# Root and reciprocal of the latent norms on one column per token tile, spread by TensorE between two halves of the next projection

## What is computed

```python
def rms_norm(x, g=None):
    xf = x.astype(jnp.float32)
    y = xf * lax.rsqrt(jnp.mean(xf * xf, axis=-1, keepdims=True) + NORM_EPS)
    if g is not None:
        y = y * g.astype(jnp.float32)
    return y.astype(x.dtype)
...
qh = (rms_norm(cq, g_mla_q) @ w_mla_qb).reshape(B, T, MLA_HEADS, MLA_NOPE + MLA_ROPE)
...
kvh = (rms_norm(ckv, g_mla_kv) @ w_mla_kvb).reshape(B, T, MLA_HEADS, MLA_NOPE + MLA_V)
...
k_pe = jnp.broadcast_to(rope_2d(kr[:, :, None, :], tabs_mla), (B, T, MLA_HEADS, MLA_ROPE))
```

## Time and profile before

| | |
|---|---|
| median of 3 runs | 3298.01 us (3291.66 to 3300.49) |
| profiled execution, its own time | 3290.88 us |
| its span, first to last instruction | 3289.1 us |
| PE matmuls busy | 3118.7 us (95%) |
| PE weight loads busy | 2624.0 us (80%, beside the matmuls) |
| DVE busy | 1486.3 us (45%) |
| ACT busy | 1169.0 us (36%) |
| POOL busy | 399.6 us (12%) |
| mean granted clock of TensorE | 0.985 |

### The profile page before, as it was taken

One profiled execution on the slowest core, in us unless ns is written; L12 is line 12 of the kernel. 1 busy time (PEld: TensorE's weight loads), 2 busy tenths in 40 slices (PEclk: granted clock), 3 DMA queues, 4 the chain that ended last, 5 costly groups with the idle time before them and its releaser, 6 DMA issues.

```text
span 3289.1 us, 42671 instructions
## 1 busy us (share of the span) xinstructions
PE 3118.7 (95%) x17576; PEld 2624.0 (80%) x17576; DVE 1486.3 (45%) x2013; ACT 1169.0 (36%) x1709; POOL 399.6 (12%) x304
## 2 busy tenths in 40 slices
PE   6899999999999999999999988999999999999998
PEld 5788888899888877787888867788788877778886
DVE  5555524444436644422222356554455456443334
ACT  3344423444424422211111234443355444332222
POOL 0011100111102201010100100111022112010101
PEclk9999999999999999999999999999999999999999
DMA  4111142111152244124233342223222232422323
GB/s 178 67 54 59 62 139 76 60 59 63 53 175 68 83 135 135 58 88 129 64 122 96 111 134 70 65 64 93 84 78 74 91 121 82 133 83 96 96 96 102
DMA packets 99827, 303.96 MB, mean 92 GB/s; under 512 B 10960, under 2 KB 23376, under 8 KB 99664
## 3 DMA queue, kind: packets, MB, share of 16 engines
q1 hardware_dynamic: 54720, 190.34, 18.1%
q10 hardware_dynamic: 44944, 111.32, 10.2%
HBM read 271.73 MB, written 29.88 MB: 92 GB/s over the span
## 4 chain that ended last, share of the span: by engine, by line
PE 77%; issue 9%; DVE 8%; ACT 4%; POOL 1%; DMA 1%; ACTq 0%; DVEq 0%; POOLq 0%
PE ps L1518 72%; PE ps L1606 2%; PE ps L1644 1%; DVE wl L979 1%; POOL ptl L1500 1%; ACT wh L492 1%; DVE tmp L984 1%; DVE mx L1005 1%; DVE ptl L1020 1%; DVE tmp L1155 1%; DVE hl L1164 0%; PE ps L1722 0%; PE ps L1576 0%; ACT pth L528 0%; ACT prob L540 0%
## 5 line engine op out<-in xcount | busy, mean ns | idle before, releaser
L1518 PE MATMUL ps<-hh,wh 128*128 128x512 f32 x2768 | 831.7, 361 | 41.7 <-DVE wl L979 20.4
L1518 PE MATMUL ps<-hl,wh 128*128 128x512 f32 x2768 | 813.8, 354 | 0.0
L1518 PE MATMUL ps<-hh,wl 128*128 128x512 f32 x2768 | 811.0, 353 | 0.0
L979 DVE TENSOR_TENSOR wl<-raw,wh 128x1024 fp32r<-128x1024 f32 (+2 forms) x356 | 466.0, 1310 | 523.8 <-ACT wh L492 514.3
L1518 PEld LDWEIGHTS ps<-hh,wh 128*128 128x128 f32 x2768 | 451.2, 190 | 127.1 <-issue 35.4
L492 ACT ACTIVATE wh<-raw 128x1024 fp32r<-128x1024 f32 (+2 forms) x356 | 362.2, 1018 | 429.1 <-PE ps L1518 376.4
L1518 PEld LDWEIGHTS ps<-hh,wl 128*128 128x128 f32 x2768 | 451.5, 189 | 77.5
L1518 PEld LDWEIGHTS ps<-hl,wh 128*128 128x128 f32 x2768 | 452.7, 190 | 74.2 <-issue 0.7
L1518 PE MATMUL ps<-yh,wh 128*128 128x512 f32 (+1 forms) x1296 | 403.0, 365 | 14.2 <-DVE yl L1380 5.4
L1518 PE MATMUL ps<-yl,wh 128*128 128x512 f32 (+1 forms) x1296 | 395.5, 359 | 0.0
L1518 PE MATMUL ps<-yh,wl 128*128 128x512 f32 (+1 forms) x1296 | 391.4, 356 | 0.0
(11 more groups left out here) (209 smaller groups left out, 3269.9 us busy)
## 6 DMA issues: line engine op xcount, KB each, us to landing
raw<-in_stream SPq DMA_DIRECT2D x328, 512.0 KB, 3.6
prob<-in_wmod ACTq DMA_DIRECT2D x40, 512.0 KB, 3.6
mraw<-in_wmod ACTq DMA_DIRECT2D x36, 512.0 KB, 3.8
gspill<-prob ACTq DMA_DIRECT2D x32, 384.0 KB, 2.3
tmp<-gspill ACTq DMA_DIRECT2D x24, 384.0 KB, 3.1
early_y<-in_wmod SPq DMA_DIRECT2D x12, 512.0 KB, 14.2
vraw<-gspill ACTq DMA_DIRECT2D x16, 384.0 KB, 3.8
dec<-in_dec ACTq DMA_DIRECT2D x8, 768.0 KB, 4.3
```

What stands on the lines that cost most here:

```text
L979: dve.tensor_tensor(wl[:, s, 0:n], raw[:, s, 0:n], wh[:, s, 0:n].bitcast(F32), ALU.subtract).then_inc(sem("w_lo"), 1)
L1518: ins = pe.matmul(out, lhs[w], rhs[x](cols), start=start and n == 0, stop=stop and n == 2)
```

## The change

The sums of squares go to one column per token tile (`squares`): the 12 matmuls of 128 tokens (8 for layer 1's query) have the squares as weights and one column of ones as the moving side. ACT takes the root of 128 x 6 numbers into `qsc`, DVE their reciprocal. PE spreads the result back over the partitions (`broadcast`): one matmul for each token tile, whose weights are the tile's column repeated 128 times and whose moving side is the identity, into `pair(AUX)`. DVE waits for it (`v_bc`), and its scaling reads `pair(AUX)` in place of `tmp`. PE's program is rewritten: `broadcast` of the query stands between the two halves of chunk 2's projection, `broadcast` of key/value between chunks 4 and 5. Its `squares` for key/value also wait for `v_norm`, since they write where the scaling of the query reads.

```diff
--- before.py
+++ after.py
@@ -143,7 +143,7 @@
             phase("summed", layer, 0, {}, summed, nt=TOK)
             phase("norm", layer, 0, {}, norm, nt=TOK, first=True)
         phase("mla_in", layer, 0, {}, total(
-            {"chunk": 6, "free0": 3, "free1": 2, "v_stat": 2, "v_std": 2, "v_rstd": 2,
+            {"chunk": 6, "free0": 3, "free1": 2, "v_stat": 2, "v_std": 2, "v_rstd": 2, "v_bc": 2,
              "v_norm": 4, "v_hi": 6, "v_lo": 6, "tab": 1}, ROPED))
         head = total({"chunk": 1, "free0": 1}, ROPED)
         att = attention(nq)
@@ -745,7 +745,10 @@
                                            ACT.Square).then_inc(sem(f"free{k}"), 1)
                         if j:
                             split(at, 5)
-                        std(at, j, nt_j, MLA_RANK)
+                        nq = nt_j // P
+                        act.wait_ge(sem("v_stat"), at.v("v_stat", j + 1))
+                        act.activation(qsc[:, j, 0:nq], pair(AUX)[:, 0:nq], ACT.Sqrt, bias=eps[:, :],
+                                       scale=1.0 / MLA_RANK).then_inc(sem("v_std"), 1)
                         if j:
                             split(at, 6)
                         for k in range(RKT):
@@ -1232,13 +1235,16 @@
                                 split(at, 2 * j + k + 1)
                         if j:
                             split(at, 5)
-                        rstd(at, j, nt_j)
+                        nq = nt_j // P
+                        dve.wait_ge(sem("v_std"), at.v("v_std", j + 1))
+                        dve.reciprocal(qsc[:, j, 0:nq], qsc[:, j, 0:nq]).then_inc(sem("v_rstd"), 1)
                         if j:
                             split(at, 6)
+                        dve.wait_ge(sem("v_bc"), at.v("v_bc", j + 1))
                         for k in range(RKT):
                             col = g0 + 2 * KT + j * RKT + k
                             dve.scalar_tensor_tensor(out=tmp[:, k, 0:nt_j], in0=tmp[:, k, 0:nt_j],
-                                                     scalar=gains[:, col:col + 1], in1=tmp[:, 2, 0:nt_j],
+                                                     scalar=gains[:, col:col + 1], in1=pair(AUX)[:, 0:nt_j],
                                                      op0=ALU.mult, op1=ALU.mult).then_inc(sem("v_norm"), 1)
                         for k in range(RKT):
                             dve.wait_ge(sem("v_norm"), at.v("v_norm", 2 * j + k + 1))
@@ -1776,15 +1782,37 @@
                     spread(at, nt)
 
                 elif kind == "mla_in":
-                    for j, nt_j in enumerate((TOK if layer < DEPTH - 1 else LAT, TOK)):
-                        if j == 0 and layer:
-                            project_pair(at, nt_j)
-                        for k in range(RKT if j else 0):
-                            project(at, 2 * j + k, k, j, H, KT, nt_j, whole)
+                    def squares(j, nt_j):
+
                         for k in range(RKT):
                             pe.wait_ge(sem(f"free{k}"), at.v(f"free{k}", j + 1))
-                        stats(at, prob, (0, 1), nt_j, j)
+                        if j:
+                            pe.wait_ge(sem("v_norm"), at.v("v_norm", 2))
+                        for k in range(RKT):
+                            for q in range(nt_j // P):
+                                ins = pe.matmul(pair(AUX)[:, q:q + 1], prob[:, k, q * P:(q + 1) * P], ones[:, 0:1],
+                                                start=k + q == 0, stop=k == RKT - 1 and q == nt_j // P - 1)
+                        ins.then_inc(sem("v_stat"), 1)
+
+                    def broadcast(j, nt_j):
+
+                        pe.wait_ge(sem("v_rstd"), at.v("v_rstd", j + 1))
+                        for q in range(nt_j // P):
+                            ins = pe.matmul(pair(AUX)[:, q * P:(q + 1) * P], qsc[:, j, q:q + 1].to_broadcast([P, P]),
+                                            ident[:, :], start=True, stop=True)
+                        ins.then_inc(sem("v_bc"), 1)
+
+                    nt_q = TOK if layer < DEPTH - 1 else LAT
+                    if layer:
+                        project_pair(at, nt_q)
+                    squares(0, nt_q)
+                    project(at, 2, 0, 1, H, KT // 2, TOK, whole, ktn=KT, done=False)
+                    broadcast(0, nt_q)
+                    project(at, 2, 0, None, H, KT // 2, TOK, whole, kt0=KT // 2, ktn=KT)
+                    project(at, 3, 1, 1, H, KT, TOK, whole)
+                    squares(1, TOK)
                     project(at, 4, 0, 2, H, KT // 2, TOK, whole, ktn=KT, piece=True)
+                    broadcast(1, TOK)
                     project(at, 5, 0, None, H, KT // 2, TOK, whole, kt0=KT // 2, ktn=KT, piece=True)
 
                 elif kind in ("mla_first", "gqa_first"):
```

## The result

The changed kernel takes 3304.35 us (median of 12 runs, 3301.53 to 3309.21) against 3296.93 (12 runs, beside it) for the one before. The medians are 7.4 us apart, 0.23%; the ratio is 1.0027, with a 95% interval of 1.0020 to 1.0034, so the kernel is slower beyond noise, by less than 0.3%, the bound of the forecast's likely cases. The profiled execution has a span of 3300.7 us.

A forecast was written before the change was run, and what follows sets the result against it. TensorE's dense projections were taken to bound the kernel. The chain terms summed to 0.0 us at unchanged clock and clock falls added +3.5, giving 3301.5 us on the median of 3298.01, range 3293 to 3307.

The forecast's parts named there:

- the forecast's likely cases: Whole kernel: the likely cases were all put within 0.3% of the time before; chance of "same" 0.92.
- The reciprocals: On VectorE: 4.96 us falls to 0.19; some 5 us saved per site, swallowed in layer 0's query by the half projection.
- The sums: On TensorE: 24 one-column records take 2.5 us against 2.46; nothing won for 768 tokens, 0.3 lost for 512.
- The spread: On TensorE, inside the next projection: six matmuls add 1.3 us, four 0.9; bounds 0.7 and 2.6.
- Layer 1's query: VectorE scales 1.3 us later, so chunk 3 too: loss 1.3; a clock fall, called a toss-up, adds 0.7.
- The clock: TensorE's clock falls to half behind one-column sums: +1.4 us per key/value site, together +3.5 over all sites.
- the price of a fall: 1.4 us, from layer 0's chunk 3 projection: 9.99 us with a fall, 8.57 for its twin in layer 1.
- the balance that I had set to zero: Layer 0's query: clock low longer under thinner sums (+1.4 us), against the fall before chunk 3 going (-1.4).
- with thinner ones it stays low longer: Layer 0's query sums: the clock, already low from 67.8 to 71.2, stays low longer, +1.4 us.
- The clock doesn't care: Rival, chance 0.35: all sites keep full clock; change 0.0 or -1.4 us, time 3296.6 to 3298.
- the reciprocals come off whole: Rival, chance 0.04: the spread doesn't hold VectorE back; 4.96 us leaves the chain at three sites, -15 us, 3283.
- dear spreads: Rival, chance 0.03: loading one column read 128 times is slow on TensorE; slower by 9.9 us.

The follow-up runs named there:

- short_recip: Kernel before the change, with this phase's reciprocal on only 6 (4) columns, other tokens left out, no spread: 3288.05 us, ratio 0.9976.
- wide_double: wide_sums with every spread run twice: 3298.41 us, ratio 1.0004 to the kernel before, 0.0021 over wide_sums.
- wide_again: wide_sums timed a second time, no further edit: 3292.99 us, ratio 0.9990 to the kernel before.
- again: The changed kernel timed a second time, no edit: 3301.73 us, ratio 1.0016 to the kernel before.
- kv_only: Only key/value by the new form (one-column sums, spread), query as in the kernel before: 3301.08 us, ratio 1.0013.
- wide_kv: kv_only with 128-column sums, query as in the kernel before: 3292.88 us, ratio 0.9992.
- wide_sums: Changed kernel, its sums moving 128 columns of ones instead of one, loops swapped: 3290.8 us, ratio 0.9983 to the kernel before.
- wide_mix: wide_sums with layer 1's query as it was before the change: 3291.36 us, ratio 0.9983 to the kernel before.
- Wide_early: Changed kernel with 128-column sums and each spread behind the next projection's first tile instead of the fourth: 3293.9 us, ratio 0.9994.

## Why the prediction was right, and where a size was off

The range held the time (3304.35 in 3293 to 3307), and the direction was right. The forecast was +3.5 us, 3301.5 on the median, and +7.4 came, twice as much. Of the 3.9 us between them the time shows only 2.9, since the median of before, with more runs, came down from 3298.01 to 3296.93.

*The reciprocals.* That their 5 us per site would be swallowed by the half projection ahead of the spread is shown: DVE scaled in layer 0 10.06 us after the sums began against 10.14 before. short_recip gives the other side: without a spread the saving is 8 us, not the 15 that the chain's shares suggest, and by the estimate in the table above half of it is less time at the low clock.

*The sums.* 2.5 us were put down for 24 records, 2.67 came (67.06 to the projection at 69.73). At full clock the chain's gain at key/value was 0.39 instead of 0.6 (16.26 to 15.87), most of it for this reason.

*The spread.* 1.3 us predicted, 1.26 to 1.35 measured, and wide_double's 1.33 more for the second one. The bound of 2.6 fell away.

*Layer 1's query.* A later chunk 3 by 1.3 us at full clock: wide_again, which had no fall there, took 22.02 us against 20.79, 1.2 more.

*The clock.* At the key/value sums the mechanism was right: behind one-column sums the clock fell every time, and behind 128 columns in their place it never did, at the same duration. The step that was mis-sized is the price of a fall. I took 1.4 us from chunk 3's projection in layer 0. Here a stretch with a fall cost 1.5 to 4.7 us over the 15.87 of one without, 3.1 in the mean of six (19.02 - 15.87), since low stretches of 3.4, 6.8 and, in `again`, 10.2 us occurred. With 3.1 for 1.4 and 0.4 for 0.6 the two key/value sites give 5.5 instead of 1.6. That is the 3.9 us that the forecast lacked. At the two query sites the errors (+0.6 in layer 1, -0.6 in the mean in layer 0) cancelled, which is luck. Layer 1's query cost 2.6 us in both profiles (20.79 to 23.39), where 1.3 + 0.7 were put down: the fall that was a toss-up came. At layer 0's query the balance that I had set to zero came out at -1.4 and 0.0 in the two profiles. The saved half of it held: with the old gap of 2.4 to 2.6 us before chunk 3 the clock fell there in three of three profiles (before, kv_only, wide_kv), with the new one of about 1 us in none of seven. The other half, "with thinner ones it stays low longer", held in `again` (6.8 us instead of 3.4) and not in the first profile (3.4 as before).

*The rivals.* "The clock doesn't care" is refuted by the pair wide_kv and kv_only and by wide_sums against `again`, "the reciprocals come off whole" by the chain, "dear spreads" by their duration.

*What stays open.* The stretches of the phase explain the changed kernel's loss, but not all that the wide forms gain. In wide_sums' profile they add up to +0.6 us against before, in wide_again's to -0.9, in wide_mix's to -2.2, while the medians say -5.5, -2.3 and -3.9, with 3 us to either side. The mean clock of all runs accounts for these gains (the table above), within its error, so what is missing lies in falls outside the four stretches, or in executions that have no profile. Where they are wasn't settled: in the changed kernel's profile layer 1's projections from 2007.51 on, behind the phase, took 9.48 us for 36 records with a fall of 3.4 us in them, and 7.88 before, and such falls come and go from profile to profile. Wide_early has the shortest stretches of all kernels that spread (76.7 us in the sum of the four, against 80.9 in wide_sums' profile) and isn't the fastest. Its runs spent 11 us more at the low clock than those of wide_sums, by the estimate 5 us of time, and its profile shows no fall in the four stretches. Why the low time is longer elsewhere is open.

## What to carry to other kernels

Work that leaves an engine is worth what the next engine gets to start sooner: here a result handed back by TensorE had to wait its turn in TensorE's own order, and 5 us of saved reciprocal became next to nothing (0.4 us at key/value at full clock). Before moving it, ask where in that order the answer will stand, and what the same saving is worth if it needed no answer (short_recip: 8 us). And a matmul of one column cost as much here as one of 128, its weights changing each time, while the clock fell behind it more often; where such sums follow an idle stretch, try moving more columns. Here that took off 7 us (key/value only) to 11 us (all four places).

## What the runs showed of the hardware that was not expected

- 12 matmuls with changing f32 weights took 2.81 us with one moving column and 2.92 with 128 (PE's rows, tails included).
- Behind the key/value sums, which follow 1.65 to 1.69 us of idle time, the granted clock fell to 0.50 with one-column sums in eight of eight cases, with 128-column sums in none of twelve and with the old sums, which move 512 and 256 columns, in none of six. At layer 0's query sums, after 1.92 to 1.96 us of idle time, it fell with all three forms (4 of 4, 3 of 5, 3 of 4). PE was busy throughout such a fall (6.80 of 6.80 us behind the key/value sums of the changed kernel's layer 0). They lasted 3.4 to 10.2 us, and each us at 0.50 cost 0.44 to 0.47 us.
- The spread, whose weights are one column read 128 times over, takes 0.11 us a record like the transposes of the earlier trace rows, but has two records a matmul and they have one: six matmuls took 1.35 us.
